# Moving the hidden-state loads to another issuing queue, and six memsets to VectorE, in a two-layer hybrid encoder

## The reference, cut to what matters

```python
for l in range(DEPTH):                                    # 2 layers, 1040 tokens, width 1024
    mix = hybrid_mixer(rmsnorm(h, g_mix_pre[l]), ...)     # RG-LRU and gated linear attention
    h = h + rmsnorm(mix, g_mix_post[l])
    x = rmsnorm(h, g_mlp_pre[l])
    ff = square(relu(x @ w_up[l])) @ w_down[l]            # 1024 -> 4096 -> 1024
    h = h + rmsnorm(ff, g_mlp_post[l])
```

## Time and profile before

| | |
|---|---|
| median of three runs | 2353.68 us (2351.77 to 2360.39) |
| the profiled execution | 2351.77 us, its span 2350.0 us |
| TensorE busy | 2245.5 us, 96% of the span |
| VectorE busy | 1650.2 us, 70% |
| mean granted TensorE clock | 0.986 |
| middle groups, layer 0 | 556 to 1090 us |
| middle groups, layer 1 | 1728 to 2244 us |

### The profile page before, as it was taken

One profiled execution on the slowest core, in us unless ns is written; L12 is line 12 of the kernel. 1 busy time (PEld: TensorE's weight loads), 2 busy tenths in 40 slices (PEclk: granted clock), 3 DMA queues, 4 the chain that ended last, 5 costly groups with the idle time before them and its releaser, 6 DMA issues.

```text
span 2350.0 us, 34547 instructions
## 1 busy us (share of the span) xinstructions
PE 2245.5 (96%) x13856; PEld 2029.5 (86%) x13856; DVE 1650.2 (70%) x1638; ACT 698.7 (30%) x828; POOL 624.4 (27%) x387
## 2 busy tenths in 40 slices
PE   7999999999989999999999999999999999999997
PEld 7999889998989989999989999877777777777787
DVE  6788544664867867867587886436749679769768
ACT  4564332440211211211244643333402211211212
POOL 3333215023122222123414332150232222122240
PEclk9999999999999999999999999999999999999999
DMA  3111002456454454441241110033564643643514
GB/s 134 34 56 36 28 28 90 125 190 230 145 188 164 153 197 156 151 174 70 83 138 43 50 42 32 28 99 110 183 235 143 216 163 121 224 178 126 186 55 144
DMA packets 122673, 290.73 MB, mean 124 GB/s; under 512 B 9552, under 2 KB 29264, under 8 KB 122576
## 3 DMA queue, kind: packets, MB, share of 16 engines
q10 hardware_dynamic: 81568, 155.09, 18.9%
q1 hardware_dynamic: 41008, 134.28, 16.8%
HBM read 251.25 MB, written 38.08 MB: 123 GB/s over the span
## 4 chain that ended last, share of the span: by engine, by line
PE 71%; DVE 14%; DMA 7%; issue 4%; ACT 2%; POOL 1%; DVEq 0%; ACTq 0%; SPq 0%; POOLq 0%
PE banks L793 29%; PE banks L1063 16%; PE banks L1033 9%; PE banks L924 5%; DMA r<-w_units 3%; DMA X<-t_mem 3%; PE banks L845 2%; DVE w_hl L2251 1%; PE banks L848 1%; DMA w_raw<-w_units 1%; DVE sum_lo L2282 1%; DVE hid L2269 1%; DVE w_third L2251 1%; PE banks L833 1%; PE banks L832 1%
## 5 line engine op out<-in xcount | busy, mean ns | idle before, releaser
L793 PE MATMUL banks<-X,w_hl 128*128 128x348 f32 (+2 forms) x3744 | 648.8, 332 | 2.4 <-ACT ki L1549 1.8
L793 PEld LDWEIGHTS banks<-X,w_hl 128*128 128x128 f32 x3744 | 605.7, 188 | 30.2 <-issue 7.5
L1063 PE MATMUL banks<-sum_hi,w_hl 128*128 128x260 f32 (+1 forms) x1440 | 316.4, 324 | 28.1 <-DVE sum_lo L2282 23.7
L1033 PE MATMUL banks<-X,w_hl 128*128 128x260 f32 (+1 forms) x1944 | 316.4, 322 | 7.4 <-DVE w_hl L2251 7.4
L1033 PEld LDWEIGHTS banks<-X,w_hl 128*128 128x128 f32 x1944 | 281.6, 190 | 37.6 <-issue 8.0
L645 POOL TENSOR_SCALAR w_hl<-w_raw 128x1024 fp32r<-128x1024 f32 x70 | 92.0, 1315 | 791.0 <-issue 528.2
L1063 PEld LDWEIGHTS banks<-sum_hi,w_hl 128*128 128x128 f32 x1440 | 226.4, 190 | 57.4 <-issue 31.1
L670 POOL TENSOR_SCALAR w_hl<-r 128x1024 fp32r<-128x1024 f32 x72 | 108.1, 1501 | 366.4 <-DVE r L2240 145.4
L647 POOL TENSOR_TENSOR w_hl<-w_raw,w_hl 128x1024 fp32r<-128x1024 f32 x70 | 201.9, 2884 | 5.8
L1063 PE MATMUL banks<-sum_lo,w_hl 128*128 128x260 f32 (+1 forms) x720 | 192.4, 322 | 0.0
L1621 ACT ACTIVATE hid<-banks 128x1040 f32<-128x1040 f32 (+1 forms) x48 | 49.7, 1036 | 417.0 <-PE banks L1033 417.0
(11 more groups left out here) (239 smaller groups left out, 3712.3 us busy)
## 6 DMA issues: line engine op xcount, KB each, us to landing
w_raw<-w_units SPq DMA_DIRECT2D x148, 512.0 KB, 3.5
r<-w_units SPq DMA_DIRECT2D x84, 512.0 KB, 3.9
X<-t_mem ACTq DMA_DIRECT2D x68, 520.0 KB, 6.3
X<-t_mem ACTq DMA_DIRECT2D x68, 512.0 KB, 6.2
t_extra<-t_mem ACTq DMA_DIRECT2D x22, 520.0 KB, 7.2
t_extra<-t_mem ACTq DMA_DIRECT2D x22, 512.0 KB, 7.3
h_old<-x_in ACTq DMA_DIRECT2D x12, 348.0 KB, 3.5
h_mid<-Y ACTq DMA_DIRECT2D x12, 348.0 KB, 4.0
```

Source lines behind the costliest of these rows:

```text
L793: ins = nc.tensor.matmul(out[:, b, 0:t.width(b)], wp, xp[:, t.used(b)], start=first and n == 0, stop=last and n == 2)
L1033: ins = nc.tensor.matmul(banks[:, first + b, 0:t.block], wp, xp[:, b * t.block:(b + 1) * t.block], start=opens and (half, kk, i) == (0, 0, ...
L1063: ins = nc.tensor.matmul(out[:, m + b, :], wp, xp[:, k, b * t.block:(b + 1) * t.block], start=k == 0 and i == 0, stop=k == 1 and i == 2)
```

## The change

1. The loads of the T halves in the middle groups are issued by SP and no longer by ACT. They are put among the raw loads at fixed places of SP's program, with the same conditions. ACT's copy of `middle_group` loses all its waits for halves, and its last group is no longer written out apart.
2. The six memsets of Z1, Z5 and Z6 move from POOL to DVE, where they stand behind all eight `down_sum` and ahead of the spreading of Y.
3. In the handover DVE does `x_sums(1)` ahead of the first `down_sum` (before: behind it), one `x_low` behind each of `down_sum` 2 to 5 (before: two behind each of 1 and 2), and the low part of UP_A11 behind the memsets and the spreading of Y (before: ahead of the last `down_sum`).
4. In a middle group DVE makes the low part of UP_A22 behind SUM_DN_S3 and SUM_DN_S2 (before: ahead of them), and the low part of X_T3 ahead of the ReLU of UP_4 (before: behind it).

```diff
 # SP, middle_group
+                sp.wait_ge(t_half_used, 4 * n + 1)
+                t_load(l, 0, T2, 1)
                 when_split(UP_S2)
                 sp.wait_ge(wsum_made, WEIGHT_SUMS * n + SUM_UP_S4 + 1)
                 raw_load(l, g, 0, 1, Q_A21)
                 when_split(UP_S4)
                 raw_load(l, g, 2, 0, Q_A22)
+                sp.wait_ge(up_done, products + UP_5 + 1)
+                t_load(l, 1, T3, 0)
+                sp.wait_ge(t_half_used, 4 * n + 2)
+                t_load(l, 2, T3, 1)
                 when_split(UP_S3)
                 raw_load(l, g, 1, 1, Q_A22)
+                sp.wait_ge(up_done, products + UP_6 + 1)
+                t_load(l, 0, T4, 0)
                 when_split(UP_A12)
                 raw_load(l, g, 3, 1, Q_A11)
                 when_split(UP_A22)
                 raw_load(l, g, 2, 1, Q_A12)
+                sp.wait_ge(t_half_used, 4 * n + 3)
+                t_load(l, 1, T4, 1)
+                if not last:
+                    sp.wait_ge(up_done, products + UP_7 + 1)
+                    t_load(l, 2, T2, 0)
                 when_split(DN_S4)
                 raw_load(l, g, 2, 1, Q_A11)
                 when_split(DN_S3)
                 raw_load(l, g, 0, 1, Q_A12)
+                for place, used in ((0, (t_half_used, 4 * n + 4)), (1, (up_done, products + PRODUCTS))):
+                    sp.wait_ge(*used)
+                    if not last:
+                        t_load(l, place, T1, place)
+                        continue
...
 # POOL, before group 1
                 pool.wait_ge(t_stored, 16 * 20 * (l + 1))
-                for z in (*Z1, *Z5, *Z6):
-                    nc.gpsimd.memset(z[:, :, :], 0.0).then_inc(z_zeroed, 1)
 # DVE, middle_group
                     relu(0, (0, 1))
-                    weights_low(g, UP_A22)
                     when_loaded(g, 3, 2)
                     when_summed(g, SUM_DN_S1)
                     weights_sum(g, SUM_DN_S3, 0, 3, 0, ALU.subtract)
                     when_summed(g, SUM_DN_S3)
                     weights_sum(g, SUM_DN_S2, 3, 1, 3, ALU.subtract)
+                    weights_low(g, UP_A22)
...
                     weights_low(g, DN_S3)
+                    low(X_T3, t3[:, :, 0:t.width])
                     dve.wait_ge(up_done, PRODUCTS * n + UP_4 + 1)
                     V.scalar_tensor_tensor(out=by_up_blocks(l, b21), in0=up_banks(l, 0), scalar=0.0, in1=by_up_blocks(l, half_rs(l, 0)),
                                            op0=ALU.max, op1=ALU.mult).then_inc(relu_made, 1)
-                    low(X_T3, t3[:, :, 0:t.width])
 # DVE, handover
                 group(0, l * NJ + J_MLP, l * COUNTED_TILES)
+                x_sums(1)
                 dve.wait_ge(h_stored, 16 * (2 * NX * l + kept.pieces))
                 for m in range(KT):
-                    if m == KT - 1:
-                        weights_low(1, UP_A11)
                     down_sum(m, l * NJ + J_MLP, True)
-                    if m == 0:
-                        x_sums(1)
-                    if 1 <= m < 3:
-                        x_low(1, 2 * m - 2)
-                        x_low(1, 2 * m - 1)
+                    if 2 <= m < 6:
+                        x_low(1, m - 2)
+                dve.wait_ge(t_stored, 16 * 20 * (l + 1))
+                for z in (*Z1, *Z5, *Z6):
+                    V.memset(z[:, :, :], 0.0).then_inc(z_zeroed, 1)
...
                     V.tensor_tensor(out_quarter(l, 1, 0, h), out_quarter(l, 1, 0, h), out_quarter(l, 1, 1, h), ALU.subtract).then_inc(y_spread, 1)
-                first_up_sum(1)
                 dve.wait_ge(z_zeroed, 6 * (l + 1))
                 dve.wait_ge(y_spread, 2 * (l + 1))
+                weights_low(1, UP_A11)
+                first_up_sum(1)
```

More of the change, by code:

```diff
@@ L542, in middle_group @@
             def middle_group(l, g, last):
-                n = groups_before(l, g)
+                n, products = groups_before(l, g), PRODUCTS * groups_before(l, g)
                 def when_split(operand):
                     sp.wait_ge(wpart_ready, OPERANDS * n + operand + 1)
+                sp.wait_ge(t_half_used, 4 * n + 1)
+                t_load(l, 0, T2, 1)
                 when_split(UP_S2)
@@ L563, in middle_group @@
                 raw_load(l, g, 0, 1, Q_A12)
+                for place, used in ((0, (t_half_used, 4 * n + 4)), (1, (up_done, products + PRODUCTS))):
[3 more added lines that the diff above has]
+                        continue
+                    for s in range(2):
+                        sp.dma_start(t_slot(l, place, s).bitcast(f32), b12_part(l, place, s)).then_inc(b12_loaded, 16)
                 when_split(DN_A11)
@@ L1602, in hidden, with middle_group @@
                     nc.scalar.activation(act_hi[:, i, c], T[2 + i % 2][:, c], ACT.Copy).then_inc(a_hi, 1)
-                def middle_group(g, last):
+                def middle_group(g):
                     n = groups_before(l, g)
[L1608 to L1616, removed]
                     def copied(product, chain, q):
@@ L1638, in middle_group @@
                     copied(UP_1, 0, (0, 0))
-                    when_half_used(1)
-                    t_load(0, T2, 1)
                     copied(UP_5, 1, (1, 0))
-                    t_load(1, T3, 0)
-                    when_half_used(2)
-                    t_load(2, T3, 1)
                     copied(UP_6, 0, (0, 1))
-                    t_load(0, T4, 0)
                     square(0, (0, 1))
-                    when_half_used(3)
-                    t_load(1, T4, 1)
                     copied(UP_7, 0, (1, 1))
-                    if not last:
-                        t_load(2, T2, 0)
                     square(1, (1, 1))
@@ L1657, in middle_group @@
                     square(3, (1, 0))
[L1658 to L1665, removed]
                     high(X_B11, quarter(l, (0, 0)))
@@ L1711, in _ @@
                 store_lows(1)
-                with act.Fori(1, MIDDLE) as g:
-                    middle_group(g, False)
-                middle_group(MIDDLE, True)
+                with act.Fori(1, GROUPS - 1) as g:
+                    middle_group(g)
                 act.wait_ge(h_stored, 16 * (2 * NX * l + out.pieces))
```

## The result

The changed kernel is slower: 2392.58 us median of 4 runs (2387.88 to 2397.24) against 2356.48 us of 4 runs of the kernel before on the same chip (2351.77 to 2360.39). The ratio is 1.0154, with a 95% interval of 1.0124 to 1.0184. The forecast was 2374, its range ended at 2388. The profiled execution took 2391.82 us with a span of 2390.1, 40.1 more than that of before, at a mean granted clock of 0.975 (before 0.986).

The account below looks back on a forecast made before the run. PE, busy 96%, sets the time. Handover +24 and middle groups -3 give +21 on the profiled 2351.8 us, 2373; the median lies 1.9 above that execution, so 2374, range 2350 to 2388.

Parts of the forecast that it names:

- The T2 load: Middle groups: on SP the pair stands ahead of both raw loads, lands in 5.2 us, and UP_6's stall goes.
- The handover: Once a layer, DVE's program sets when PE goes on; 11.8 us idle ahead of UP_1, +24 us in all.
- the x_sums: Handover: placed ahead of the first down_sum they make job 2 wait 5.9 us; +4 us in each layer.
- The six memsets: Handover: on DVE behind the last job, with PE's next instruction waiting on them; 1.15 us each, 6.9 us for six.
- The price of UP_A22's new place: Middle groups: raw 2's issue now waits behind two more sums; 2.5 us, taking back most of the freed queue's gain.
- DVE's chain through raw 2: Middle groups: down products start when this chain ends, not when UP_4 ends; 8.9 us from raw 2's landing.
- the term at raw 1: Middle groups: nine loads, 4.7 MB, from t=10.1 take 12.1 us at 0.39 MB/us, so raw 1 lands at 22.3.
- A forecast gain of 0.9 us in each group: Middle groups: first down product at t=44.5 in place of a mean of 45.4; twelve groups give 10 us.
- the 7 us that were forecast for the clock and the ReLU: Middle groups: 4 us of lost clock over all twelve, 3 us for layer 0's ReLU of UP_4 being held up.
- Rival 3: Middle groups: one queue congests, raw 2 at t=37.5 or later, clock lost in every group; +14 +24, 2390 us; chance 0.13.

Follow-up runs that it names:

- e2: Kernel before with only the handover changes (memsets on DVE, x_sums first, late low part of UP_A11): 2375.43 us, ratio 1.0091.
- e12: Kernel before with only the x_sums ahead of the first down_sum and the x_low moved; memsets stay on POOL: 2363.64 us, ratio 1.0040.
- e10: Kernel before with one line moved, the low part of UP_A22 behind SUM_DN_S3 and SUM_DN_S2: 2385.63 us, ratio 1.0135.
- e5: Changed kernel with T4's second half issued on SP ahead of the wait for UP_A22 and raw 2: 2394.45 us, ratio 1.0177.
- e4: Changed kernel with the low part of UP_A22 back ahead of the two sums: 2348.64 us, ratio 0.9974.
- e6: Changed kernel with the six memsets back on POOL: 2380.05 us, ratio 1.0114.
- e7: Changed kernel with the low part of X_T3 back behind the ReLU of UP_4: 2385.06 us, ratio 1.0141.
- e9: Changed kernel with the middle groups' T loads back on ACT: 2405.54 us, ratio 1.0228.
- e1: Kernel before with only the middle groups' T loads moved to SP: 2327.79 us, ratio 0.9882.
- e3: Kernel before with only the low parts of UP_A22 and X_T3 at their new places: 2384.32 us, ratio 1.0129.
- e8: Kernel before with T loads on SP, raw 1 ahead of T3's second half, T4's second half ahead of raw 2: 2318.33 us, ratio 0.9856.
- e11: Kernel before with T loads on SP, raw 1 ahead of T3's second half, raw 2 still ahead of T4's second half: 2295.14 us, ratio 0.9756.

## Why the prediction was wrong

**Right.** The T2 load is served earlier, its pair landing 6.0 us after the first issue (5.2 forecast), and UP_6's stall is all but gone. The handover costs about what was said: 11.5 us of idle against 11.8, and +21 in e2 against +24, of which e12 gives the x_sums +9 against +8. The six memsets run at a pitch of 1.09 us, 6.5 in all, against 6.9. The Trainium skill ("VectorE: DVE Perf Modes", Zero memsets can be issued as uint32) gave 1.08 for each, an estimate that the trace confirms. The price of UP_A22's new place with the queues as they were, 2.5 us a group, is what e10 measured: 2.5. And DVE's chain through raw 2 decides when the down products start, not the T4 load: e5 removed the one stall and the other took its whole length.

**Right in size only: the x_sums.** Their +9 against +8 is in part luck. Job 2 waits 3.5 us in layer 0 and not 5.9, because the x_sums took 6.2 us there and not the 8.5 of the forecast, which rests on the row of 5.03 in the earlier trace rows. The down jobs begin 1.9 us later than before (506.84 against 504.89), but that cancels: ACT's scaling begins 2.0 us later as well (512.19 against 510.18), and PE is already 2.0 us late near 443 us, in a part that the change leaves alone. The traces show what goes with the length. The last four x_sums of this half take 5.6 to 5.8 us where most of POOL's second splitting instruction (L667, before L647) runs beside them (layer 0 of e4, e6, e7 and e9, layer 1 of e12) and 2.9 to 3.7 where little or none of it does (both layers of the changed kernel, of e2 and of e5); job 2 waits 5.8 to 6.3 us in the first case and 1.9 to 3.6 in the second. So the forecast had priced one of two cases, and in layer 0 shifts of under 1 us between ACT's scaling, POOL's splitting and the down jobs went with the one or the other. That POOL's instruction is the cause of the longer rows is argued from these traces; no run moved it.

**Wrong: the term at raw 1.** The step "they take 12.1 us at 0.39 MB/us ... It lands at 22.3" is the one that failed. Raw 1 was there at 23.9. The rate was that of a burst under way; the first six microseconds moved 279, 320 and 342 GB/s in turn, the next eight 399, 400, 393 and 395. Added up from these windows, an estimate, the 4.7 MB had moved at t=23.0, 0.7 after the forecast's 22.3, and the load counted as landed 0.9 later still, a term that the sum did not have. The window of 401 GB/s came from late in a burst; the earlier ones of the same burst, 379, 328 and 380, were in the trace of before and would have given part of it. The sum behind it ran in 1.71 us and not 1.23, and from there each step was as forecast: raw 3 after 3.6 us (3.5), 3.7 us of DVE work, raw 2 after 3.6 (3.5), 8.9 to the first down product. (For the 3.5 us no row was at hand; that it came out is luck.)

So the whole chain was 2.3 us late, 46.8 against 44.5. A forecast gain of 0.9 us in each group became a loss of 1.5, which is +15 over the ten counted groups. The first group of each layer, which also holds what the handover changes, has its first down product at t=49.7 and 50.6, against 47.7 and 47.1 in e2, the handover alone: another +5.5. With the handover's 21 this is 42 us, and the spans differ by 40 and the ratios by 36, so nothing is left over to explain. The clock lost behind the T4 stall lies ahead of the first down product and is within the 15, and from the first down product to the next group's start the ten groups take only 0.7 us more in all; the 7 us that were forecast for the clock and the ReLU are not there as a separate loss. As a sum: 2.3 us in twelve groups are 28, the handover gives back 3 and these two terms 6, and 19 is what the median lies above the forecast.

**What the account of UP_A22 missed.** The prediction priced its place at 2.5 us, the two sums that it now stands behind. With the queue freed there is also DVE's wait for raw 3 (1.37 us in the row of 1882.63), in which the instruction had lain at no cost in e1 and e4. Between e4 and the changed kernel the first down product moves by 3.9 us, not 2.5. The prediction's own numbers held this: from 24.8, with 2.4 us of other DVE work, the early low part would have ended at 28.4 and the late one at 32.1, 3.7 apart. It took the 2.5 from a row of the old order instead. That left the forecast of the whole alone, but hid that part 1 by itself was a clear gain and that the single move of one instruction turned it into a loss.

**The parts and their sum.** Alone they are worth -27.8 (e1), +21.4 (e2) and +30.4 (e3), in sum +24.0; the change cost +36.3. The 12 us between lie at the meeting of parts 1 and 4: without part 4's UP_A22 the rest adds up (-28 + 21 is -7, e4 shows -6), and beside it part 1 gains 17 and not 28. In the changed kernel SP waits for UP_A22 from t=27 to 34, with T4's second half behind that wait, so a late low part delays a load that has nothing to do with it; but e5 put that load ahead of the wait and gained nothing, so the 12 us are not there. They lie in the place of UP_A22 itself: with the T loads on ACT it costs 2.5 us a group (e10), with them on SP 3.9 (e4), because there its early place is free. 1.4 us in twelve groups are 17, an estimate that covers the 12. Rival 3, 2390 us for "one queue congests", was the case that came, by its condition too (raw 2 at 37.9, "37.5 or later"); it was given 0.13 and the range stopped 4.6 us short of the median. Its price of 14 us for the middle groups is what the ratios leave beside e2 (36 less 21 is 15). Its name is half right: raw 1 does land 3.5 us later than before in the single queue, but it does so in e1 too, which is 28 us faster than before.

**One queue or two.** Raw 2 is the clearest case. On SP's queue beside ACT's T4 pair it was there 6.7 us after the low part that lets it go; ahead of the pair in one queue 3.9 at most (e1); behind the pair 5.7 after its issue (e8). The Trainium skill ("DMA: Bandwidth & Descriptors", Queues, rings and completion order) says that a DMA engine alternates between the queues with work and takes each in order. All three agree with that. The prediction used this only to price what raw 1 loses, not for what raw 2 gains when it is put ahead; e11 against e8 shows this at 24 us, and part 1 with both raw loads ahead (e11) at -57 in place of -28.

Left open: why PE is 2.0 us late by 443 us, ahead of all that the change touches; whether POOL's splitting is what lengthens the x_sums; and whether the X_T3 move costs anything.

## What to carry to other kernels

When transfers move into another engine's queue, write down the new queue as one list in order, and for each entry both what it now waits behind and what waits behind it: the loads were better there (e1), which of them stood ahead was worth up to 30 us (e11 against e1), and how late one wait of that list ended was worth 42 (e4). Look at a stall as a chain and not as a row: the largest wait of the changed kernel (55.8 us for the T load) was worth nothing, and one instruction of 1.2 us that no wait of PE names directly was worth 42. Try the parts of a change one by one; one that loses can hide another that gains.

## What the runs showed of the hardware

In the changed kernel a burst of loads on one queue moved 279, 320 and 342 GB/s in its first three stretches of 2 us and 399 afterwards, at a DMA share of 0.95 and more throughout, so there the share does not tell how fast it moves. Other bursts have their low stretch elsewhere: before, 379, 328, 380 and 392 in turn, and in e1 391, 331, 363 and 405. A memset row of DVE lasts 0.93 us for 1040 columns while the next starts 1.09 later, so six such rows add up to 5.6 us and take 6.4. Four x_sums of 520 columns take 3.67 us on DVE (changed kernel) and 5.62 with POOL's L667 beside them (e6).
